# FOX values with the values held still, a reordered first quad and shifted SBUF addresses in a two-layer fp32 decoder

## The reference

```
def modulate(x, w, shift, scale):
    return rmsnorm(x, w) * (1 + scale[:, None, :]) + shift[:, None, :]

for i in range(DEPTH):
    mod = c_act @ w_mod[i] + b_mod[i]
    sh1, sc1, g1, sh2, sc2, g2 = jnp.split(mod, N_MOD, axis=-1)
    h = modulate(x, norm1_w[i], sh1, sc1)
    y = hgrn2_mixer(...) if i % 2 == 0 else fox_mixer(...)
    x = x + g1[:, None, :] * y
    h = modulate(x, norm2_w[i], sh2, sc2)
    x = x + g2[:, None, :] * ((relu(h @ w1) ** 2) @ w2)

# fox_mixer, 16 heads of 64, for each block of 128 queries
s = einsum('bhqd,bhkd->bhqk', qb, k) * scale + (Fq[..., :, None] - F[..., None, :])
p = softmax(where(kpos <= qpos, s, -inf))
o = einsum('bhqk,bhkd->bhqd', p, v)
return (o * sigmoid(g)) @ w_out
```

## Time and profile before

| what | value |
|---|---|
| median of 3 runs | 1428.87 us (1428.7 to 1429.33) |
| the profiled execution | 1429.67 us |
| its span, first to last instruction | 1427.9 us |
| mean granted TensorE clock | 0.988 |
| TensorE busy | 1393.0 us (98%) |
| VectorE, ScalarE, POOL busy | 760.6 us (53%), 501.0 us (35%), 159.1 us (11%) |
| weight blocks | 208 of 512 KB |

### The profile page before, as it was taken

One profiled execution on the slowest core, in us unless ns is written; L12 is line 12 of the kernel. 1 busy time (PEld: TensorE's weight loads), 2 busy tenths in 40 slices (PEclk: granted clock), 3 DMA queues, 4 the chain that ended last, 5 costly groups with the idle time before them and its releaser, 6 DMA issues.

```text
span 1427.9 us, 21924 instructions
## 1 busy us (share of the span) xinstructions
PE 1393.0 (98%) x8184; PEld 1207.8 (85%) x8184; DVE 760.6 (53%) x1342; ACT 501.0 (35%) x772; POOL 159.1 (11%) x206
## 2 busy tenths in 40 slices
PE   6899999999999999999999999999999999999997
PEld 4779898989988888888899998998898888888887
DVE  7664757564776446663356555555556432344333
ACT  5613242413443212432236454544335321233220
POOL 7151505050000000000001101010000000000000
PEclk8999999999999999999999999999999999999998
DMA  9433333321265456553214122212123322323311
GB/s 378 162 126 119 134 122 129 119 75 59 96 244 181 150 201 220 189 191 102 89 60 149 60 90 73 91 60 70 46 78 103 98 93 88 103 88 91 99 60 59
DMA packets 47496, 169.44 MB, mean 119 GB/s; under 512 B 5168, under 2 KB 7344, under 8 KB 46912
## 3 DMA queue, kind: packets, MB, share of 16 engines
q1 hardware_dynamic: 46816, 164.21, 33.8%
q10 hardware_dynamic: 608, 4.23, 0.8%
HBM read 166.29 MB, written 2.13 MB: 118 GB/s over the span
## 4 chain that ended last, share of the span: by engine, by line
PE 91%; DVE 5%; ACT 2%; issue 1%; DMA 1%; POOL 0%; SPq 0%; POOLq 0%; DVEq 0%; ACTq 0%
PE bank L761 22%; PE bank L762 21%; PE bank L763 21%; PE bank L861 3%; PE bank L862 3%; PE bank L863 3%; PE bank L932 3%; PE bank L1142 2%; PE bank L1112 1%; PE bank L1128 1%; PE bank L951 1%; DVE modf L1344 1%; DVE wlo L1291 1%; DVE scr L1266 1%; PE bank L1165 1%
## 5 line engine op out<-in xcount | busy, mean ns | idle before, releaser
L356 ACT ACTIVATE whi<-raw 128x1024 fp32r<-128x1024 f32 x204 | 215.3, 1055 | 264.8 <-PE bank L763 254.6
L1291 DVE TENSOR_TENSOR wlo<-raw,whi 128x1024 fp32r<-128x1024 f32 x205 | 252.5, 1245 | 16.7 <-ACT whi L356 16.7
L699 POOL TENSOR_TENSOR rst<-ssq,mhalf 128x8 f32<-128x8 f32 (+2 forms) x29 | 42.3, 1468 | 1129.1 <-DVE ssq L1244 944.9
L1552 DVE TENSOR_TENSOR scr<-scr 128x512 f32<-128x512 f32 x64 | 44.3, 692 | 126.7 <-ACT scr L526 126.7
L761 PE MATMUL bank<-h3hi,whi 128*128 128x512 f32 (+1 forms) x288 | 107.6, 374 | 1.1 <-DVE h3lo L1271 1.0
L761 PE MATMUL bank<-h1hi,whi 128*128 128x512 f32 (+1 forms) x288 | 106.8, 371 | 0.9 <-DVE h1lo L1271 0.6
L762 PE MATMUL bank<-h3lo,whi 128*128 128x512 f32 (+1 forms) x288 | 107.2, 372 | 0.0
L763 PE MATMUL bank<-h3hi,wlo 128*128 128x512 f32 (+1 forms) x288 | 107.2, 372 | 0.0
L761 PE MATMUL bank<-a0hi,whi 128*128 128x512 f32 (+1 forms) x288 | 106.5, 370 | 0.0
L763 PE MATMUL bank<-a0hi,wlo 128*128 128x512 f32 (+1 forms) x288 | 106.5, 370 | 0.0
L762 PE MATMUL bank<-a0lo,whi 128*128 128x512 f32 (+1 forms) x288 | 106.5, 370 | 0.0
(11 more groups left out here) (255 smaller groups left out, 3183.6 us busy)
## 6 DMA issues: line engine op xcount, KB each, us to landing
raw<-stream SPq DMA_DIRECT2D x208, 512.0 KB, 4.1
mring<-mod_rows SPq DMA_DIRECT2D x80, 512.0 KB, 3.6
modf<-mod_rows SPq DMA_DIRECT2D x16, 512.0 KB, 15.2
fb<-negf ACTq DMA_DIRECT2D x4, 1024.0 KB, 5.6
x<-x_t SPq DMA_DIRECT2D x4, 512.0 KB, 5.9
out_t<-x SPq DMA_DIRECT2D x8, 256.0 KB, 2.2
wf<-w_forget SPq DMA_DIRECT2D x1, 512.0 KB, 5.0
par<-params SPq DMA_DIRECT2D x1, 86.0 KB, 2.0
```

The costliest lines, as they stand in the source:

```text
L356: S.activation(whi[:, j, :], raw[:, j, :], ACT.Copy).then_inc(w_hi, 1)
L699: G.tensor_tensor(rst[:, at:at + n], ssq[:, at:at + n], mhalf[:, 0:n], ALU.pow).then_inc(done, 1)
L1291: V.tensor_tensor(wlo[:, j, :], raw[:, j, :], whi[:, j, :].bitcast(F32), ALU.subtract).then_inc(w_lo, 1)
L1552: V.tensor_tensor(scr[j % 2][:, :], scr[j % 2][:, :], scr[j % 2][:, :], ALU.mult).then_inc(ff_sq, 1)
```

## The change

1. **First quad.** For k from 3 on, VectorE computes the shift's `row_dot` first, then the normed x, the low part of k-1, and last the gain, which now signals `h_t`; for k up to 2 the order is changed likewise. ScalarE waits for the same things by fewer semaphores.
2. **Values.** They run for a pair of units at once, after the odd one. `vt` (64 columns) is held still, `pT` (128 queries) streams, and the two heads of a pair go to the column halves of the array, head b into partitions 64b to 64b+63 of `ps[2]`. The output is already features by queries: `turn_o`, `heads_out` and `ot_tr` go. The division comes before the transposes instead: `scaled(c)` on VectorE takes the reciprocal of one unit's sums and multiplies `prob` in place; transposes now wait for it (`s_n`). `ot` shrinks to 128x512 and takes the first half's output by one copy a step (`half_out`).
3. **Last step.** `FPIECES` gives 19 slices of the output product to the slots instead of 16, and five instead of eight follow them; the low parts of two weight blocks are made at u = 6 and 7, two slots later than before.
4. **Addresses.** Two unused tiles, 128 and 64 bytes per partition, move the activations of both layers to a multiple of 256 bytes plus 192. `whi` and `wlo` stay at plus 128.

```
+        sb("spacer0", [P, 32], F32)
...
+        sb("spacer1", [P, 16], F32, layer0)
...
-        ot = sb("ot", [P, TT, GW], F32, fox)
+        ot = sb("ot", [P, T], F32, fox)
...
-        FPIECES = [0, 0, 0, 2, 0, 2, 1, 2, 1, 1, 1, 1, 1, 1, 1, 2]
+        FPIECES = [0, 0, 0, 2, 0, 2, 1, 2, 1, 2, 1, 2, 1, 2, 1, 2]
...
             def transposes(s, u):
                 c = UNITS * s + u
-                pe.wait_ge(s_p, c + 1)
+                pe.wait_ge(s_n, c + 1)
...
-            def values(s, u):
-                f, i, b = unit(u)
-                pe.wait_ge(s_pt, UNITS * s + u + 1)
...
-                for t in range(i + 1):
-                    mm = PE.matmul(ps[2][:, o0:o0 + DH], cols(pT[:, u % 2, :], t),
-                                   vt[:, t, v0:v0 + DH], start=t == 0, stop=t == i, skip_group_check=True)
+            def values(s, pair):
+
+                f, i, _ = unit(2 * pair)
+                pe.wait_ge(s_pt, UNITS * s + 2 * pair + 2)
...
                 for t in range(i + 1):
+                    for b in range(2):
+                        v0 = GW * (s % 2) + DH * (2 * f + b)
+                        mm = PE.matmul(ps[2][DH * b:DH * b + DH, P * i:P * i + P], vt[:, t, v0:v0 + DH],
+                                       cols(pT[:, b, :], t), start=t == 0, stop=t == i, skip_group_check=True)
                 mm.then_inc(s_pv, 1)
-
-            def turn_o(s, units_done):
-
-                pe.wait_ge(s_o, 2 * s + 2)
-                pe.wait_ge(s_pt, units_done)
-                for f in range(2):
-                    for t in range(TT):
-                        mm = PE.transpose(cols(ps[2 - f], t), cols(ot[:, t, :], f), ident[:, :])
-                    mm.then_inc(ot_tr, 1)
...
-                    if u >= 1:
-                        values(s, u - 1)
-                values(s, UNITS - 1)
-
-            w_out_begin(L + Q_OUT, y1, done, done + 4)
-            turn_o(GROUPS - 1, UNITS * GROUPS)
-            w_out_begin(L + Q_OUT, y1, done + 4, 4 * EARLY)
+                    if u % 2:
+                        values(s, u // 2)
+
+            w_out_begin(L + Q_OUT, y1, done, 4 * EARLY)
...
+            for k in range(SCALES, KT):
+                row_dot(SH1 + k)
                 normed_0(k).then_inc(x_n, 1)
...
+                lower_0(k - 1)
+                dve.wait_ge(scale_sum, k + 1 - SCALES)
+                first_gain(k, mod[:, SC1 + k:SC1 + k + 1]).then_inc(h_t, 1)
             lower_0(KT - 1)
...
+            def scaled(c):
+
+                u = c % UNITS
+                n = P * (unit(u)[1] + 1)
+                over = rst[:, 32 + u:33 + u]
+                dve.wait_ge(s_p, c + 1)
+                link(V.reciprocal(over, den[:, c:c + 1]))
+                V.tensor_scalar(prob[:, u % 2, 0:n], prob[:, u % 2, 0:n], over, None, ALU.mult).then_inc(s_n, 1)
+
+            def half_out(s):
+
+                dve.wait_ge(s_pv, UNITS // 2 * s + TT)
+                V.tensor_copy(ot[:, :], ps[2][:, :]).then_inc(s_o, 1)
...
-                        lower_ahead(n - 1)
-                        if n == 4 * L + 31:
-                            lower_ahead(n)
+                        if (s_, b) != (GROUPS - 1, 1):
+                            lower_ahead(4 * L + 6 + 8 * s_ + b - 1)
+                    if s == GROUPS - 1 and u in (2 * TT - 2, 2 * TT - 1):
+                        lower_ahead(4 * L + 32 + u - 2 * TT)
```

More of the change, by code:

```diff
@@ L153, in build @@
         n_sum, n_var, n_rst, n_bc = (sem(n) for n in ("n_sum", "n_var", "n_rst", "n_bc"))
-        h_32, x_n, s_g = sem("h_32"), sem("x_n"), sem("s_g")
+        h_32, x_n = sem("h_32"), sem("x_n")
         h_t, h_hi, h_lo = (sem(n) for n in ("h_t", "h_hi", "h_lo"))
@@ L171, in build @@
             sem(n) for n in ("f_var", "f_rst", "f_nrm", "f_tr", "f_te", "f_lo"))
-        s_pe, s_ns, s_p, s_tr, s_pt, s_pv, s_rd, s_o = (
-            sem(n) for n in ("s_pe", "s_ns", "s_p", "s_tr", "s_pt", "s_pv", "s_rd", "s_o"))
-        ot_tr = sem("ot_tr")
+        s_pe, s_ns, s_p, s_n, s_tr, s_pt, s_pv, s_o = (
+            sem(n) for n in ("s_pe", "s_ns", "s_p", "s_n", "s_tr", "s_pt", "s_pv", "s_o"))
         fy_t, fy_hi, fy_lo = (sem(n) for n in ("fy_t", "fy_hi", "fy_lo"))
@@ L400, in upper_0 @@
                 if k >= 2:
-                    act.wait_ge(s_g, k - 1)
                     act.wait_ge(h_lo, k - 1)
@@ L1124, in transposes @@
                     pe.wait_ge(fx_v, 2)
-                if s and u == 1:
-                    pe.wait_ge(fy_t, 2 * s)
                 for t in range(unit(u)[1] + 1):
@@ L1204, in between @@
                             turn(*turn_of(s, u))
-                    elif s and u == 0:
-                        def between():
-                            turn_o(s - 1, UNITS * s + 1)
                     if s == u == 0:
@@ L1358, in _ @@
             normed_0(0).then_inc(x_n, 1)
-            for k in range(1, KT):
-                normed_0(k).then_inc(x_n, 1)
[L1361 to L1371, removed]
+            row_dot(SH1 + 1).then_inc(h_t, 1)
+            normed_0(1).then_inc(x_n, 1)
+            lower_0(0)
+            normed_0(2).then_inc(x_n, 1)
+            lower_0(1)
+            link(row_dot(SC1 + 2))
+            first_gain(2, mod[:, SC1 + 2:SC1 + 3])
+            row_dot(SH1 + 2).then_inc(h_t, 1)
+            for k in range(SCALES, KT):
+                row_dot(SH1 + k)
+                normed_0(k).then_inc(x_n, 1)
+                lower_0(k - 1)
+                dve.wait_ge(scale_sum, k + 1 - SCALES)
+                first_gain(k, mod[:, SC1 + k:SC1 + k + 1]).then_inc(h_t, 1)
             lower_0(KT - 1)
@@ L1613, in turned @@
                 if c >= 2:
-                    dve.wait_ge(s_pv, c - 1)
+                    dve.wait_ge(s_pv, c // 2)
                 V.tensor_copy(pT[:, u % 2, 0:n], ps[1][:, 0:n]).then_inc(s_pt, 1)
@@ L1623, in turned_low @@
                                        op1=ALU.subtract).then_inc(f_lo, 1)
[L1625 to L1638, removed]
+            def scaled(c):
[8 more added lines that the diff above has]
+                V.tensor_copy(ot[:, :], ps[2][:, :]).then_inc(s_o, 1)
             def gated(s):
+                dve.wait_ge(f_gate, s + 1)
                 for f in range(2):
-                    dve.wait_ge(ot_tr, 2 * s + f + 1)
-                    dve.wait_ge(f_gate, s + 1)
-                    V.tensor_tensor((acc, sqb)[f][:, :], ps[2 - f][:, :], gs[:, f, :], ALU.mult).then_inc(fy_t, 1)
+                    if f:
+                        dve.wait_ge(s_pv, UNITS // 2 * s + 2 * TT)
+                    V.tensor_tensor((acc, sqb)[f][:, :], (ot, ps[2])[f][:, :], gs[:, f, :], ALU.mult).then_inc(fy_t, 1)
             def y_lower(s):
@@ L1669, in _ @@
             biased(1)
+            scaled(0)
             lower_ahead(4 * L + 4)
@@ L1676, in _ @@
                         biased(c + 1)
[L1677 to L1680, removed]
+                    if u % 2 == 0:
+                        scaled(c + 1)
                     turned(s, u)
@@ L1694, in _ @@
                     for s_, b in ended(s, u, FENDS):
-                        n = 4 * L + 6 + 8 * s_ + b
-                        lower_ahead(n - 1)
-                        if n == 4 * L + 31:
-                            lower_ahead(n)
+                        if (s_, b) != (GROUPS - 1, 1):
+                            lower_ahead(4 * L + 6 + 8 * s_ + b - 1)
+                    if s == GROUPS - 1 and u in (2 * TT - 2, 2 * TT - 1):
+                        lower_ahead(4 * L + 32 + u - 2 * TT)
                     if turn_of(s, u):
                         turned_low(*turn_of(s, u))
-            heads_out(GROUPS - 1, 1)
+                    if u == 2 * TT:
+                        half_out(s)
             gated(GROUPS - 1)
```

11 lines of the change are left out of this document (5 added, 6 removed).

## The result

The changed kernel takes 1395.55 us (median of four runs, 1394.23 to 1399.09) against 1428.78 us: a ratio of 0.9773, 95% interval 0.9758 to 0.9788. That is 33.2 us less, where 23.5 were forecast. The profiled execution is the slowest of the four, 1399.09 us, with a span of 1397.4; its differences by stage are read with that in mind.

A forecast was written before the change was run, and what follows sets the result against it. TensorE was taken as the bound, busy 1393.0 of 1427.9 us, except in the first quad (VectorE's and ScalarE's order). Terms gave -15.7 without addresses, -23.5 with them: 1405.4 us from 1428.87, range 1385 to 1427.

The forecast's parts named there:

- Addresses: Both layers' activations at offset 64 from `whi`: 512-column matmuls at 231.2 ns, -7.8 us; bounds -25.7 and +27.4.
- First quad: Chain through VectorE and ScalarE: a k falls from 4.65 to 3.1 us, -6.0 us; bounds -9.3 and -3.
- Values: FOX's values in column halves running together, 7.3 us a step, 29.0 instead of 35.2 in all: -6.2 us.
- turning: FOX's output transposes and the wait for `ot` go, 0.2 given back for `half_out`: -4.0 us.
- stall: Scaling `prob` on VectorE lengthens a unit's chain; covered in steps 0 to 2, +0.5 us in the last step.
- 0.35 a pair: Values in FOX: entering and leaving the column-half form costs 0.35 us for both switches, 2.8 us a step.
- the forecast's 1345: Sign for the addresses: windows of the MLPs should hold 1345 matmuls in 311 us.
- A: Rival, addresses: the offset frees most of the surcharge, -41.4 in all, 1387.5 us, 1372 matmuls a window; chance 0.18.
- B: Rival, addresses: the offset changes nothing, 1413.2 us; chance 0.14.
- C: Rival, FOX's values: column halves run one after the other, +11.6 instead of -6.2, 1423.2 us; chance 0.17.
- D: Rival, addresses: an offset of 64 is the worst, all 3648 matmuls at 240 ns, 1440.6 us; chance 0.09.

## Why the prediction was right or wrong

The direction, and the four places, were right, and 1395.55 us lies in the range. The gain was 9.7 us larger than forecast, and 8 to 9 of that are one term.

- **Addresses, -7.8 forecast, -16 to -17 measured: the term that was mis-sized.** The forecast drew a line through 232.1 ns at a distance of 128 and 233.0 at 192 and read off 231.2 at 64. It is 228.9 there, 3.5 ns under layer 0's and 4.4 under layer 1's value: 2016 x 3.5 + 1632 x 4.4 = 14.2 us by estimate, where 4.7 were forecast; the forms of 256 columns carry the rest. Of those the token-major ones, forecast at 0.6, give 384 x 3.4 + 1152 x 2.3 ns = 4.0 us. No line is hidden in these numbers: at 32 the cost is that of 192. That the distance decides, and not the remainder, was right.
- **First quad, -6.0 forecast, -8.3 measured.** The chain of the earlier trace rows was the right one. The forecast gave a k 3.1 us, since it put ScalarE's three operations and 0.3 of hand-overs one behind the other, and took 1.7 off for what might come late. A k takes 2.87: ScalarE's operations follow one another closely, and only the way from the gain to the next `scr` costs 0.3. That is about TensorE's own 2.8, and nothing came late: the end of the range where TensorE is the limit was the nearer one.
- **Values, -6.2, turning, -4.0, and stall, +0.5; together -9.7.** No run takes them apart, but the table of FOX's records does: 9.2 us less in all, and the medians give 17.3 - 8.3 = 9.0. The records cost 0.055 as forecast. With the 5.5 us that come back in the weight matmuls the values are worth -7.4; the forecast, with 0.35 a pair for its own two switches, priced these too high and did not see that the one into the scores would move and not go. The turning is worth -3.3. The transposes of `prob` take 1.6 more, of which the waits that the profile names are 0.3 at most; the rest is in part a switch again (the first transpose behind a values group takes 0.165 us). VectorE's 46.2 us against 45 is as good. The waits are as small as 0.3 only thanks to the last step's edits, which the forecast gave no term of their own: the run with the values alone, without them, has 3.1 us of waits in the last step and is only 4.9 us faster than before. That 9.2 is so near to 9.7 is in part luck: the three terms missed by 1.2, 0.7 and 1.1 us, and not all to one side.
- **Sum.** Without the addresses 15.7 were forecast and 17.3 measured, with them 23.5 and 33.2. The MLPs' windows have 1344 matmuls in 307 us, which would be 1360 in 311: between the forecast's 1345 and A's 1372.

The rivals: B (addresses worth nothing) fell with the runs that move only them. The Trainium skill, "SBUF — State Buffer", section "Who interferes with whom", by which TensorE's two read ports are independent and it never waits on anyone, speaks of other engines and has no cost by address. Here the same instructions go at 226.7 or at 233.3 ns by the distance of their two operands alone; whether the two reads meet each other is not shown. C (column halves one after the other) fell with the pairs of starts 6 to 7 ns apart. The Trainium skill, "TensorEngine Tiling (Array Packing)", section "When to Use Tiling", gave a factor of 2 for the swap, by the prediction's estimate 17.6 us less. The records' sum went from 35.2 to 22.3, and 5.5 us of that come back ahead of these groups and of the scores. The section "Key Properties" of that page of the Trainium skill says that a change of mode drains the engine; the 0.21 and 0.33 us ahead of a group, instead of 0.12 and 0.23, agree with it. D (64 is the worst distance) fell: of those measured it is the second best for 512 columns. A had a value that exists, in the wrong place: 226.7 ns is found at a distance of 0, and there the 256-column form goes at 119.9 and not at 113.

## What to carry to other kernels

- Where TensorE has no gaps, read the distance from start to start of equal matmuls in different stages; a difference of even 0.4% between stages that do the same is a question to settle with two unused tiles before any schedule is touched. A line through two such values is no forecast: put one run at each multiple of 64 bytes (the two others tried here, 32 and 96, were as slow as the slowest).
- Of a matmul with one side of 64, hold that side still and give the two heads to the column halves, in turn and not one after the other; then see what the operation that has moved into the chain (here the division) delays, and keep filler work in those slots. Count the changes of form over the whole stream: one that stood between two small forms does not go when something else is put between them.
- In a chain through two engines, move what does not depend on the hand-over in front of it; the gain ends where the next engine's own time begins, and here that was at 2.8 us a k.

## What the runs showed of the hardware

- A matmul of 512 columns in fp32r takes 226.7, 228.9, 232.4 or 233.3 ns from start to start by the distance of its two operands modulo 256 bytes, as a mean over hundreds of matmuls, alike in two MLPs with DMA shares of 0.5 and 0.3. The order over the distances (0, 64, 128, then 32, 96 and 192 alike) is only described by this; what in the reads makes it was not found.
- At a distance of 64 the form of 256 columns goes at 113.3 ns in some stretches and at 117.8 in others: of layer 0's `a0` the first two thirds at 113.3 and the last at 117.8 with the addresses alone, and all at 117.8 in the changed kernel, with the same remainders. At 192 both values occur too. What selects between them stays open; it is worth 0.6 us for these 128 matmuls.
- TensorE begins records for the free column half ahead of older ones for the busy half: ahead of exactly three, in groups of 8, 12 and 16 records (second row of starts at 14, 275 and 494 ns), as far as the starts tell the heads apart.
- Going into a form with another division of the array costs 0.09 us over the record's own price, and so does leaving it (0.203 instead of 0.109).
